# TensorE's feed-forward loop over chunks is written out as straight code

## The reference, cut to what matters

```
D_MODEL = 2048                                   # D_FF = 5632
def swiglu(h, wg, wu, wd):
    return (jax.nn.silu(h @ wg) * (h @ wu)) @ wd

mix = merge_heads(attn_o, hg_o, hg, hg_norm_g[l], w_out[l])
x = layer_norm(ALPHA * x + mix, ln1_g[l], ln1_b[l])
x = layer_norm(ALPHA * x + swiglu(x, w_gate[l], w_up[l], w_down[l]), ln2_g[l], ln2_b[l])
```

## Time and profile before

| | |
|---|---|
| time, median of 3 runs | 2788.77 us (2787.93 to 2790.07) |
| the profiled execution | 2790.04 us, span 2788.5 us |
| TensorE matmuls busy | 2680.1 us, 96% of the span |
| VectorE, ScalarE, GpSimd busy | 1241.4, 792.2, 198.1 us |
| mean granted TensorE clock | 0.974 of full speed |
| matmuls | 21531 |
| instruction packets (queue 8) | 161, 2.64 MB |

### The profile page before, as it was taken

How to read it: one execution, slowest core, us unless ns; L and a number is a source line. 1 busy time by engine, 2 the same in 40 slices (tenths; PEclk the granted TensorE clock), 3 DMA queues, 4 the chain that set the end, 5 groups by cost and what they waited for, 6 DMA issues and landing times.

```text
span 2788.5 us, 49457 instructions
## 1 busy us (share of the span) xinstructions
PE 2680.1 (96%) x21531; PEld 2611.8 (94%) x21531; DVE 1241.4 (45%) x1794; ACT 792.2 (28%) x1194; POOL 198.1 (7%) x214
## 2 busy tenths in 40 slices
PE   5999999999999999889999999999999999999996
PEld 5989999999998889879999999999999999999995
DVE  5156777776666414563323232323232323232347
ACT  6243344332334212352121212121112121112124
POOL 1111112110000220020000000000000000000002
PEclk9999999999998989999999999999999999999998
DMA  4322333333221332312323232323232323232321
GB/s 132 102 61 79 98 84 91 91 92 93 69 73 56 108 91 69 91 46 91 92 92 91 92 91 92 91 92 91 92 91 92 91 92 91 92 91 92 91 77 62
DMA packets 341220, 243.56 MB, mean 87 GB/s; under 512 B 7208, under 2 KB 310616, under 8 KB 340504
## 3 DMA queue, kind: packets, MB, share of 16 engines
q1 hardware_dynamic: 333696, 218.97, 26.9%
q0 software_dynamic: 7344, 21.80, 2.7%
HBM read 229.43 MB, written 11.31 MB: 86 GB/s over the span
## 4 chain that ended last, share of the span: by engine, by line
PE 93%; DVE 4%; ACT 2%; issue 1%; DMA 0%; SPq 0%; DVEq 0%; ACTq 0%
PE acc L1096 81%; PE b L1080 2%; PE acc L1118 1%; DVE lnd L2006 1%; PE b L1359 1%; PE b L1241 1%; DVE wl L1539 1%; PE b L1334 1%; PE b L1438 1%; ACT wh L600 1%; PE b L1257 1%; PE b L1416 1%; PE b L1269 0%; PE b L1360 0%; DVE xl L2014 0%
## 5 line engine op out<-in xcount | busy, mean ns | idle before, releaser
L1096 PE MATMUL acc<-xh,wh 128*128 128x260 f32 (+2 forms) x4896 | 1012.8, 288 | 28.0 <-issue 14.8
L1096 PE MATMUL acc<-xl,wh 128*128 128x260 f32 (+2 forms) x4896 | 999.3, 286 | 0.0
L1096 PE MATMUL acc<-xh,wl 128*128 128x260 f32 (+2 forms) x4896 | 995.5, 285 | 0.0
L1539 DVE TENSOR_TENSOR wl<-raw,wh 128x2048 fp32r<-128x2048 f32 (+1 forms) x201 | 461.3, 2296 | 975.7 <-ACT wh L600 958.8
L1096 PEld LDWEIGHTS acc<-xh,wh 128*128 128x128 f32 (+1 forms) x4896 | 762.3, 191 | 37.1 <-issue 16.9
L1096 PEld LDWEIGHTS acc<-xh,wl 128*128 128x128 f32 (+1 forms) x4896 | 766.7, 191 | 0.0
L1096 PEld LDWEIGHTS acc<-xl,wh 128*128 128x128 f32 (+1 forms) x4896 | 763.3, 191 | 0.0
L600 ACT ACTIVATE wh<-raw 128x2048 fp32r<-128x2048 f32 x200 | 382.5, 1913 | 1211.8 <-PE acc L1096 1208.7
L1096 PE MATMUL acc<-hh,wh 128*128 128x260 f32 x1408 | 285.4, 284 | 3.2 <-DVE hl L2031 2.2
L1096 PE MATMUL acc<-hh,wl 128*128 128x260 f32 x1408 | 283.6, 283 | 0.0
L1096 PE MATMUL acc<-hl,wh 128*128 128x260 f32 x1408 | 282.6, 282 | 0.0
(11 more groups left out here) (375 smaller groups left out, 1968.5 us busy)
## 6 DMA issues: line engine op xcount, KB each, us to landing
raw<-in_w_in_dram SPq DMA_DIRECT2D x52, 1024.0 KB, 5.5
raw<-in_w_gate_dram SPq DMA_DIRECT2D x44, 1024.0 KB, 5.5
raw<-in_w_up_dram SPq DMA_DIRECT2D x44, 1024.0 KB, 5.5
raw<-in_w_down_dram SPq DMA_DIRECT2D x44, 1024.0 KB, 5.1
raw<-in_w_out_dram SPq DMA_DIRECT2D x16, 1024.0 KB, 5.6
xtok<-in_x_prompt_dram SPq DMA_DIRECT2D x4, 1024.0 KB, 8.8
ss<-in_state_hgrn_dram POOLq DMA_DIRECT2D x8, 512.0 KB, 4.8
out_dram<-ss POOLq DMA_DIRECT2D x8, 512.0 KB, 3.9
```

Of the source, the lines that this page charges most:

```text
L1096: ins = mm(acc[0:rows, t.odd, half, 0:n_], a, b[:, kx0 + k, lo + half * n_:lo + half * n_ + n_], start=(k == 0 and n == 0), stop=(k == kt ...
L1539: V.tensor_tensor(wl[:, s.odd, 0:n], raw[:, s.odd, 0:n], fr(wh[:, s.odd, 0:n]), ALU.subtract)\
```

## The change

On TensorE alone, the loop of ten passes is unrolled by the Python that writes the program: `mlp(c, mlp_plan(c))` is called for c = 1 to 11 with a plain number. Then `mlp_plan` gives constants, and the semaphore values in the waits are constants and no register sums. Order, operands and number of matmuls and waits are the same. TensorE's program becomes longer by nine bodies. The programs of the other engines, their loops among them, stay.

```diff
         two_products(At(S_E), At(T_E), lambda k: pe.wait_ge(sem("x1_in"), k + 1))
         mlp(0, mlp_plan(0)[2:])
-        with pe.Fori(1, NC, 1) as c:
+        for c in range(1, NC + 1):
             mlp(c, mlp_plan(c))
-        mlp(NC, mlp_plan(NC))
         ln_sums(2)
```

## The result

The kernel with straight code took 2761.94 us in the median of 5 runs (2755.94 to 2773.22), the one before 2787.93 us (5 runs, 2784.64 to 2790.07): a ratio of 0.9915 with an interval of 0.9888 to 0.9943. The direction was right; the time lies 3 us under my range.

| | runs | median us | from, to |
|---|---|---|---|
| before | 49 | 2788.65 | 2776.54, 2796.92 |
| straight | 22 | 2768.25 | 2755.36, 2773.22 |

A forecast was written before the change was run, and what follows sets the result against it. TensorE bounds the kernel (93% of the wait chain). Nine jumps cost 21.8 us, register constants and straight-code fetching 0, so 2790.04 - 21.8 = 2768.2 us, or 2768.5 us from the median; forecast 2768 us, range 2765 to 2773 us.

The forecast's parts named there:

- The jumps' price: TensorE's feed-forward loop: nine taken branches wait for their target's code to be fetched; removing them saves 21.8 us.
- Its split: Feed-forward jumps: 21.8 us is 14.8 us idle, 4.6 us in three long passes, and 2.4 us rest.
- the three passes of 139.4 us: Feed-forward passes, 139.4 us instead of 137.85 us; clock lowered after a gap, 4.6 us in all.
- Constants for registers: Semaphore waits in the feed-forward body: constants replacing registers taken as 0, under 0.1 us either way.
- Fetching straight code: TensorE's ten straight bodies: fetches run beside matmuls and cost 0; instruction packets near 145 for 161.
- A: Straight feed-forward code: each instruction packet crossing stalls, giving 2816 us at 0.5 us each or 2921 us; chance 0.03.
- B: Feed-forward chunk borders: gaps come from a semaphore or register waits and stay, time 2788.8 us; chance 0.03.
- C: Feed-forward: part returns, as lowered clock (4.6 us, 2772.8 us) or some 0.5 us a border; chance 0.05.
- The cover at the border: Feed-forward chunk border without gap: hidden values still ready ahead of their product, nearest cover 5.0 us, so no new wait.
- those for `hl` at the end: Last feed-forward chunk: TensorE waits for hidden values, not for the jump; these 2.2 us stay.
- the likeliest case by itself: Whole kernel, jumps' price removed: reaches from 2765.5 us to 2770.5 us by stretches of lowered clock elsewhere.
- The term for the clock elsewhere: Outside the feed-forward: two stretches of lowered clock less, or one or two more, bounding the likeliest case at 2765.5 to 2770.5 us.

The follow-up runs named there:

- e2_hint: Kernel before with its loop kept and a back-edge hint added to TensorE's feed-forward loop; 2769.8 us.
- e4_nested: Kernel before, chunk loop kept, gate and up 1 to 3 made an inner loop of three passes (1536 matmuls and weight loads); 2769.00 us, ratio 0.9921.
- e3_pairs: Kernel before with five loop passes of two bodies each, four backward jumps instead of nine; 2779.44 us, ratio 0.9962.
- e6_spread_loop: Kernel before, loop kept, with the samples' value matmuls cut in two and probability transposes one step earlier; 2778.40 us, ratio 0.9972.
- e7_ten: Kernel before, chunk loop kept, inner loop of two passes over gate and up 2 and 3 (1920 matmuls and weight loads); 2790.81 us, ratio 1.0007.
- e5_spread: Straight kernel with the samples' value matmuls cut in two and probability transposes one step earlier; 2757.16 and 2758.32 us, ratios 0.9888 and 0.9901.

## Why the prediction was right in its mechanism, and the range wrong

1. The jumps' price, 21.8 us: right. The profiles' piece became shorter by that plus 1.5 us of clock; `e2_hint` and `e4_nested` get the gain with all jumps left in, `e3_pairs` half of it. That the fetch is what the branch waits for is now shown, not inferred.
2. Its split: the three passes of 139.4 us are gone with their gaps. In other profiles of looping kernels 0 of 9 (`e6_spread_loop`), 1 of 9 (`e7_ten`) and 1 of 4 gaps (`e3_pairs`) lowered the clock, so those 4.6 us belong to one execution. Without them a jump costs 1.8 to 2.2 us. The length of a gap alone doesn't decide it: before, the three gaps of 1.79 to 1.85 us did, and in `e7_ten` one of 2.13 us did not.
3. Constants for registers: 0, as taken (`e2_hint` keeps the registers and loses nothing).
4. Fetching straight code: 0, as taken. The instruction queue carried 143 packets, where I had said near 145 for the 161 of before; the nine bodies from 1286.60 to 2524.76 us take 137.57 us each, to the digit. No branch of TensorE takes over 0.24 us. Rivals A, B and C did not occur.
5. The cover at the border: it held. No wait came in place of the nine; those for `hl` at the end, 2.2 us, stayed.
6. The step that failed is "the likeliest case by itself reaches from 2765.5 us (two stretches of lowered clock less elsewhere, as the fastest run before, 2787.93 us, hints)". The term for the clock elsewhere was mis-sized: I gave it some 3 us downward from three runs, and it measures 12 us. The samples' stretch alone differs by 13.9 us between two executions, the lowest of the 49 runs before lies 12 us under their median, and the lowest of the 22 straight ones 13 us.
   - In the five runs of the result, span times mean granted clock is 2700 to 2704 us in each (2754.4 x 0.981 at one end, 2771.7 x 0.975 at the other), so their spread of 17 us is clock. Only the run of 2755.94 us has a trace; where in the program the clock fell in the other four isn't recorded.
   - That the median of these five lies 6 us under the one of all 22 is luck of the draw. So is a part of the other agreement, 2768.25 us for my 2768.0, where single runs differ by 18 us.
   - The page of before had a granted clock of 0.974, which is 2.6% of 2788.5 us or at most 72 us of lost time. I had placed 4.6 us of them in the feed-forward and did not ask whether the others would fall alike in the next run.

Why the clock falls in this block in most executions of one program and not in others isn't shown; the runs only tell that both kernels have quick and slow executions, and that the edit of `e5_spread` removes most of the difference.

## What to carry to other kernels

Look at the sequencer's branch rows of the engine that bounds the kernel: 0.2 us and 3.5 us are two kinds of loop, and the second is cured by a hint, by a shorter body or by unrolling, with the same gain (medians of 2769.8, 2769.0 and 2768.25 us). Straight code is only the bulkiest of the three. Before giving a range, split the clock's loss by stretch, and widen the range by what the stretches with small matmuls could win or lose; three runs that agree don't bound it.

## What the hardware showed that I had not expected

- A body of 1536 matmuls and weight loads is held over passes on TensorE (6 packets from 1300 to 2640 us), one of 1920 is not, and it is fetched whole (96 packets, for 105 with 2304). The Trainium skill, page "Runtime: NRT & Kernel Launch", section "Instruction fetch mechanics", gives TensorE 128 KiB, or 2048 instructions; the trace agrees with the order of size, though 1920 and some waits was too much already. The same section speaks of only two cache lines of 16 KiB and a window of two pages; `e4_nested` shows otherwise for TensorE, since 1536 of these instructions stayed held, and the measurement decides.
- A hint costs 36 ns and takes the branch from 3.53 to 0.35 us.
- TensorE's clock fell with no idle time in the profile, in a block of 24 matmuls of two columns (3.2 us). Six wide matmuls in its middle, with the transposes one step earlier, were enough to keep nine runs within 3.3 us of each other where the same program without them spreads over 18.
